# Eight changes of order and form in a two-layer fp32 decoder trunk on one Trainium2 core

## The reference, cut to what matters

```python
# layer 1
h = rmsnorm(x, a_norm) @ a_w_in                  # q, k, v, o of four heads, and 8 gate columns
gates = 15 * tanh((gates + b_gates) / 15); ig, fg = split(gates)
lf = log_sigmoid(fg)                             # = -ln(1 + exp(-fg))
b = cumsum(lf); m = running max                  # stabiliser; rows exp(b - m), exp(-m), decay per chunk
num = (q k^T * exp(D - m)) v + exp(b + m0 - m) * (C q);  C = decay * C + v k^T   # chunk after chunk
x = x + (norm(num / max(|den|, exp(-m))) * sigmoid(o)) @ a_w_out
x = x + swiglu(rmsnorm(x, ffn_norm[0]))
k2, v2 = rmsnorm(x, kv_norm) @ w_kv + b_kv       # one shared K and V, two KV heads
# layer 2
s = q k2^T / 8, band of 128;  p = exp(s - max) / (sum + exp(sink - max));  o = p v2
x = x + o @ b_w_out + b_b_out
x = x + swiglu(rmsnorm(x, ffn_norm[1])); out = rmsnorm(x, final_norm)
```

## Time and profile before

| | before |
|---|---|
| median of 3 runs | 2072.8 us (2071.33 to 2073.25) |
| the profiled execution, its own time | 2074.34 us |
| its span in the trace | 2072.7 us |
| busy in the span: PE / DVE / ACT / POOL | 2019.2 / 1349.9 / 925.3 / 1211.6 us |
| mean granted clock of PE | 0.994 of full speed |
| DMA, mean over the span | 200 GB/s |

### The profile page before, as it was taken

How to read it: one execution, slowest core, us unless ns; L and a number is a source line. 1 busy time by engine, 2 the same in 40 slices (tenths; PEclk the granted TensorE clock), 3 DMA queues, 4 the chain that set the end, 5 groups by cost and what they waited for, 6 DMA issues and landing times.

```text
span 2072.7 us, 29248 instructions
## 1 busy us (share of the span) xinstructions
PE 2019.2 (97%) x9992; PEld 1660.2 (80%) x9992; DVE 1349.9 (65%) x1929; ACT 925.3 (45%) x1951; POOL 1211.6 (58%) x1058
## 2 busy tenths in 40 slices
PE   7899999999999999999999999899999999999998
PEld 6788989878888888888878666588788888888886
DVE  7654652668777777464665677768776676645567
ACT  6444343365545545432344444536545444432233
POOL 5532520664888988565664111264888797756565
PEclk9999999999999999999999999999999999999999
DMA  5655545843777787795844000564567667688673
GB/s 154 194 189 181 184 156 203 304 133 122 254 234 258 238 255 244 252 393 169 269 136 85 28 22 22 203 213 122 176 231 251 226 229 249 213 306 313 203 257 139
DMA packets 295431, 415.03 MB, mean 200 GB/s; under 512 B 40040, under 2 KB 218232, under 8 KB 295296
## 3 DMA queue, kind: packets, MB, share of 16 engines
q1 hardware_dynamic: 260752, 307.87, 45.3%
q10 hardware_dynamic: 33120, 100.68, 13.5%
q0 software_dynamic: 1424, 4.77, 0.8%
HBM read 259.09 MB, written 154.17 MB: 199 GB/s over the span
## 4 chain that ended last, share of the span: by engine, by line
PE 86%; DVE 7%; ACT 3%; issue 2%; DMA 1%; POOL 0%; SPq 0%; ACTq 0%; DVEq 0%; POOLq 0%
PE ps L2216 21%; PE ps L2218 21%; PE ps L2217 21%; PE ps L2119 8%; PE ps L2121 4%; PE ps L2480 1%; PE ps L2339 1%; PE ps L2340 1%; PE ps L2336 1%; PE ps L2271 1%; PE ps L2509 1%; DVE mats L1652 1%; PE ps L2499 1%; DVE forms L1750 1%; PE ps L2385 1%
## 5 line engine op out<-in xcount | busy, mean ns | idle before, releaser
L2216 PE MATMUL ps<-forms,mats 128*128 128x512 f32 x2016 | 789.6, 392 | 5.5 <-ACT part L1302 2.3
L2218 PE MATMUL ps<-forms,mats 128*128 128x512 f32 x2016 | 785.9, 390 | 0.0
L2217 PE MATMUL ps<-forms,mats 128*128 128x512 f32 x2016 | 785.8, 390 | 0.0
L1007 POOL TENSOR_TENSOR mats<-sum_a,mats 128x256 fp32r<-128x256 f32 (+2 forms) x384 | 405.6, 1061 | 365.4 <-ACT mats L1241 364.4
L2216 PEld LDWEIGHTS ps<-forms,mats 128*128 128x128 f32 x2016 | 379.4, 188 | 90.8 <-issue 10.2
L2218 PEld LDWEIGHTS ps<-forms,mats 128*128 128x128 f32 x2016 | 379.3, 188 | 79.2
L2217 PEld LDWEIGHTS ps<-forms,mats 128*128 128x128 f32 x2016 | 379.5, 188 | 77.6
L1675 DVE TENSOR_TENSOR X<-ps,X 128x512 f32<-128x512 f32 x390 | 268.4, 690 | 218.4 <-PE ps L2218 216.1
L1241 ACT ACTIVATE mats<-sum_a 128x256 fp32r<-128x256 f32 (+2 forms) x392 | 201.6, 516 | 324.0 <-PE ps L2218 306.7
L1652 DVE TENSOR_TENSOR mats<-stream_raw,mats 128x256 fp32r<-128x256 f32 (+2 forms) x302 | 277.1, 919 | 18.7 <-ACT mats L1241 18.0
L1241 ACT ACTIVATE mats<-stream_raw 128x256 fp32r<-128x256 f32 (+2 forms) x302 | 156.6, 519 | 249.6 <-PE ps L2218 246.1
(11 more groups left out here) (230 smaller groups left out, 2696.2 us busy)
## 6 DMA issues: line engine op xcount, KB each, us to landing
forms<-scratch_forms ACTq DMA_DIRECT2D x182, 512.0 KB, 5.4
scratch_forms<-prep_forms SPq DMA_DIRECT2D x161, 512.0 KB, 3.5
stream_raw<-in_w_gate_up_dram SPq DMA_DIRECT2D x88, 512.0 KB, 5.4
scratch_forms<-head_forms SPq DMA_DIRECT2D x49, 512.0 KB, 2.6
scratch_hidden<-hidden SPq DMA_DIRECT2D x84, 256.0 KB, 5.5
prep_raw<-in_w_down_dram SPq DMA_DIRECT2D x38, 512.0 KB, 5.7
stream_raw<-scratch_hidden SPq DMA_DIRECT2D x32, 512.0 KB, 4.6
forms<-scratch_forms SPq DMA_DIRECT2D x28, 512.0 KB, 8.1
```

What stands on the lines that cost most here:

```text
L1007: pool.tensor_tensor(blocks(m[:, q, 1, :], it.width), stream_source(it, q), blocks(m[:, q, 0, :].bitcast(F32), it.width), ALU.subtract).th ...
L2216: mm(dst, ah, bh, start=OPENS[q] and k == 0, stop=False, skip_group_check=True)
L2217: mm(dst, ah, bl, start=False, stop=False, skip_group_check=True)
L2218: m = mm(dst, al, bh, start=False, stop=k == w - 1, skip_group_check=True)
```

## The change

1. **Start.** SP issues the eight x tiles in a row, then `a_norm`. The gate columns are issued by ACT's queue ahead of its first activation. ACT and DVE split the gate weights one tile earlier (t == 4 in place of 5).
2. **Gate chain.** The factor 15 of ig moves from DVE to ACT. A DVE `reciprocal` of the 4 x 1024 row `one_plus_exp` takes the place of ACT's Exp(-ln); it no longer waits for ACT's Ln, and an Exp of one column after the Ln loads ACT's table. The split of unit H+3 moves between ACT's Exp and Ln, and two of POOL's three gains move behind later work.
3. **First head.** No form is made behind v tile 5; forms 5 and 6 stand behind v tiles 6 and 7. DVE's low part of form 6 moves into the loop over chunks.
4. **Attention start.** An Exp of one column, ahead of the first query output, loads ACT's table.
5. **Masked copies.** The two become one of 128 x 512, over masks that lie side by side.
6. **Run B.** Its first product (six matmuls) is issued in the last pair, at s == STEPS + 1; `run(1)` goes on from the second.
7. **Seams.** At item 7 `x_normed_of` stands ahead of `stream_hi`, for both halves.
8. **Preparation.** The list `events` loses its first three products: run A spreads 84 forms over 123 products in place of 126, run B 77.

```diff
-        events = [(runs[l][8 + f].n, q) for f in range(2, 20) for q in range(NQ)]
+        events = [(runs[l][8 + f].n, q) for f in range(2, 20) for q in range(NQ)][3:]
@@ SP, start
-            for t in range(3):
+            for t in range(TT):
                 load_x(t)
-            sp.wait_ge(gate_w_cleared, 1)
-            sp.dma_start(gates[:, :, 0:NH_A], win[:, :, g0:g0 + NH_A]).then_inc(gate_w_loaded, 16)
-            sp.dma_start(gates[:, :, 32:32 + NH_A], ...).then_inc(gate_w_loaded, 16)
-            load_gains(0, a_norm[0, :])
-            for t in range(3, TT):
-                load_x(t)
+            sp.dma_start(gcol[:, 0, :], a_norm[0, :].rearrange("(k p) -> p k", p=P), ...).then_inc(a_gain_loaded, 16)
@@ POOL, gates
-            for j in range(3, 6):
-                gain(Unit(U_HEADS + j))
+            gain(Unit(U_HEADS + 3))
...
+            gain(Unit(U_HEADS + 4))
             pool.wait_ge(gate_dve, 10)
             pool.dma_start(scr_negm, negm[:]).then_inc(negm_stored, 16)
             pool.wait_ge(negm_stored, 16)
             load_neg_row(0)
+            gain(Unit(U_HEADS + 5))
@@ ACT, a run at item 7
+                        if i == 7 and q < 2:
+                            x_normed_of(it.seam[0], 2, its[i - 1].group + 4 * q, q)
...
-                            if norm < 4 and pos and q < 2:
+                            if norm < 4 and pos and q < 2 and i != 7:
@@ ACT, start
+            act.wait_ge(gate_w_cleared, 1)
+            act.dma_start(gates[:, :, 0:NH_A], win[:, :, g0:g0 + NH_A]).then_inc(gate_w_loaded, 16)
+            act.dma_start(gates[:, :, 32:32 + NH_A], ...).then_inc(gate_w_loaded, 16)
-                if t == 5:
+                if t == 4:
                     write_hi(Unit(U_GATES))
@@ ACT, gates
             act.activation(enf[:], fg[:], ACT.Exp, scale=-GATE_CAP).then_inc(gate_act, 1)
-            act.wait_ge(gate_dve, 3)
+            write_hi(Unit(U_HEADS + 3))
+            act.wait_ge(gate_dve, 2)
             act.activation(lnu[:], one_enf[:], ACT.Ln).then_inc(gate_act, 1)
-            act.wait_ge(gate_act, 2)
-            act.activation(fg[:], lnu[:], ACT.Exp, scale=-1.0).then_inc(gate_act, 1)
-            write_hi(Unit(U_HEADS + 3))
+            act.activation(table_col[:], neghalf[:, 0:1], ACT.Exp)
+            act.activation(ig[:], ig[:], ACT.Copy, scale=GATE_CAP).then_inc(gate_act, 1)
@@ ACT, first head
-                        if first and t < NQ:
-                            head_row_hi(0, t)
+                        if first and t != 5:
+                            head_row_hi(0, t - t // 6)
@@ DVE, gates
-            dve.tensor_scalar(ig[:], ig[:], GATE_CAP, None, ALU.mult).then_inc(gate_dve, 1)
...
+            dve.reciprocal(fg[:], one_enf[:]).then_inc(gate_dve, 1)
             dve.wait_ge(gate_dve, 4)
-            dve.wait_ge(gate_act, 3)
             dve.tensor_tensor(enf[:], enf[:], fg[:], ALU.mult).then_inc(gate_dve, 1)
             dve.wait_ge(gate_dve, 5)
+            dve.wait_ge(gate_act, 2)
             dve.tensor_tensor(lf[:], enf[:], lnu[:], ALU.subtract).then_inc(gate_dve, 1)
@@ DVE, attention
-                    dve.tensor_tensor(PTc[:, e % 2], pT, cur, ALU.mult).then_inc(pt_ready, 1)
-                    dve.tensor_tensor(PTp[:, e % 2], pT, prv, ALU.mult).then_inc(pt_ready, 1)
+                    dve.tensor_tensor(PT[:, e % 2], pT.unsqueeze(1).to_broadcast([P, 2, 2, P]), keep, ALU.mult
+                                      ).then_inc(pt_ready, 1)
@@ PE, a run and the attention loop
-                    for q in range(NQ):
+                    for q in range(int(l == 1 and local(it) == 0), NQ):
                         product(it, q)
...
+                if s == STEPS + 1:
+                    pe.wait_ge(bank_free[0], uses.before[0])
+                    product(runs[1][0], 0)
```

More of the change, by code:

```diff
@@ L928, in _ @@
             pool.memset(mask_neg[:], 0.0).then_inc(const_step, 1)
[L929 to L930 removed]
+            for t in (keep_le[:], keepT_cur, keepT_prev):
+                pool.memset(t, 1.0).then_inc(const_step, 1)
             pool.wait_ge(const_step, 6)
@@ L1389, in run @@
                     tile_hi(2, 3, 1)
+            act.wait_ge(gate_w_cleared, 1)
+            gates = raw[:, 0, :].rearrange("p (k n) -> p k n", k=KT)
+            g0 = 2 * NH_A * DQK + 2 * D
+            act.dma_start(gates[:, :, 0:NH_A], win[:, :, g0:g0 + NH_A]).then_inc(gate_w_loaded, 16)
+            act.dma_start(gates[:, :, 32:32 + NH_A], win[:, :, g0 + NH_A:g0 + 2 * NH_A]).then_inc(gate_w_loaded, 16)
             K = uses.stage(NORM)
@@ L1980, in head @@
                 if first:
-                    for q in range(3, NQ):
+                    for q in range(3, NQ - 1):
                         head_row_lo(0, q)
@@ L2012, in head @@
                                                      ps[:, b, 0:W1], ALU.mult, ALU.add).then_inc(bank_free[b], 1)
-                    if first and c:
-                        head_row_lo(1, c - 1)
+                    if first:
+                        head_row_lo(int(c > 0), (c - 1) % NQ)
                     if not first and not last and c < NQ:
@@ L2512, in _ @@
                             d = slice(a * DH_B, (a + 1) * DH_B)
-                            m = mm(ps[d, b, 0:P], vb[:, ne - 1, d], PTp[:, e % 2, a], start=False, stop=True)
+                            m = mm(ps[d, b, 0:P], vb[:, ne - 1, d], PT[:, e % 2, 1, a], start=False, stop=True)
                     m.then_inc(oT_ready, 1)
```

39 lines of the change are left out of this document (17 added, 22 removed).

## The result

| | before | changed |
|---|---|---|
| median | 2072.8 us (4 runs, 2071.3 to 2073.3) | 2081.3 us (4 runs, 2080.2 to 2084.5) |
| ratio of the times | | 1.0043, 95% interval 1.0031 to 1.0055 |
| the profiled execution / its span | 2074.34 / 2072.7 us | 2080.24 / 2078.6 us |
| busy PE | 2019.2 us | 2017.4 us |

The changed kernel is 8.6 us slower, where 7.9 less was forecast. Its profiled execution was the fastest of the four, and only 5.9 above that of before. Executions of one kernel spread: the fastest and the slowest lie 2 us apart in one kernel of the experiments (11) and 7.8 in another (1), and further down it is seen where.

A forecast was written before the change was run, and what follows sets the result against it. PE was taken as the bound, busy 2019.2 of 2072.7 us, leaving 53.5 for better order. Eight terms summed to -7.9: 2066.4 us for the profiled execution, 2064.9 as the median, range 2057.5 to 2070.5.

The forecast's parts named there:

- Preparation, -2.3: Runs A and B: forms three products later remove PE's 1.2 us wait for `part` in each run; -2.3 us.
- The late sum: Preparation: ACT stands 4.18 us for POOL's sum of the second prepared form, with PE's awaited copy behind it.
- Rival D: Preparation: closer pitch makes ACT wait for POOL's sum in 23 rows, 1.16 us each; slower, 2092 us; chance 0.05.
- Start, +1.9: Kernel start: `a_norm` behind eight x tiles lands at about 15.1 and delays half 1 of the gate columns; +1.9 us.
- +3.0 for a landing at 16.2: Kernel start: upper end of the start's range, if the gain vector lands at 16.2; +3.0 us.
- v copies, -3.0: First head: last v copy no longer waits behind a form's store, leaving 0.9 of wait for the state; -3.0 us.
- Gate chain, +1.8: Gates: DVE's reciprocal takes 8.4 us, scans end 1.8 later, and PE's gate wait becomes 4.5; +1.8 us.
- The rival with one pass: Gate chain: reciprocal takes one pass, 1.21 us, giving -2.7 in place of +1.8; 2060.4 us in all; chance 0.30.
- Attention start, -1.3: Attention's start: earlier table load may let DVE's scaling go before POOL's long sum; half taken, -1.3 us.
- Masked copies, -1.1: Attention: one merged copy saves 0.066 us a step, counted in the last pair's waits and six small ones; -1.1 us.
- First product, -3.9: Last pair: run B's six matmuls fill PE's gap; second product starts 3.3 ahead, 0.6 less at low clock; -3.9 us.
- Seams, 0: Seams: four forms on ACT still stand ahead of both reordered steps, so the 1.9 us wait, twice, stays; 0.

The follow-up runs named there:

- (11): Changed kernel with the old start, gate reciprocal by ACT's Exp, run A's table rejoining the old one, and form 3's low part earlier: 2066.4 us, 0.9969 to before.
- (1): Changed kernel with the old table of forms, preparation events starting three products earlier again in both runs: 2075.3 us, ratio to before 1.0007.
- table of 7: Changed kernel with run A's forms 1 to 6 at most two products later, then the old table; run B stays shifted: 2071.4 us, 0.9991 to before.
- 10: Kernel before with only run B's first product issued in the last pair: 2069.9 us, ratio to before 0.9986.

## Why the prediction was wrong

The sum of -7.9 became +5.9 in the profiled execution. Three terms are off by 15.6 together (preparation 9.3, start 3.2, v copies 3.1), and the gate chain gives 2.2 back; the rest is under 2.

- **Preparation, -2.3 became +7.0: the step that failed.** The late sum was read rightly, and the two waits for ACT's `part` went in both runs (-1.5 each). But "the pitch falls from 1.50 to 1.46 products a form, so nothing should gather" took the mean for the places. The table puts three forms on three products at six places. At five places of run A, ACT waits 3 to 4.9 for SP's store of the form two before; at two of them, where it waits 4.9 and 4.4 and the store stands behind a burst of loads, PE lost 5.3 and 4.3. Rival D had the mechanism nearly (forms that make ACT wait, with a copy of PE behind), at the wrong resource, POOL's sum in place of SP's store, and in 23 places in place of two. It had 0.05. With the old table the kernel is 6.0 faster than the changed one (1), and with the table of 7 it is 9.9 faster.
- **Start, +1.9 became +5.1 (3.8 in the mean of all).** The three queues stood as forecast. But the sum priced the gain alone, at 15.1. It landed at 15.9, and what held POOL was a load that the sum did not have, the later half of the gate columns, moved to ACT's queue, at 16.3. By the prediction's own +3.0 for a landing at 16.2, 2.1 of the 5.1 are left; beside them stands the clock after PE's 4.8 us of idleness, 0.50 and 0.67 in the two stretches behind it, which I had not counted, although the prediction itself names that price for another place.
- **v copies, -3.0 became +0.1.** The copies came when they should. The next in line was named, the state of chunk 0, and priced at 0.9; but I took it to be bound to DVE's own work. It was bound through two splits to the same store that the v copy had been taken out from behind, and form 6 as such hadn't moved. The second wait, 1.8 behind the load of the next row, was in no term.
- **Gate chain, +1.8 became -0.4.** The mechanism stands, only the sizes were off: 6.53 us where 8.4 was taken, 5.2 ns more an element and not 7, and `one_plus_exp` took 0.68 where 1.2 was taken. So the wait for the gates is 2.2 and not 4.5. The up to 2 us that POOL's split could have added to DVE's second row did not come: that row took 1.21. (The row of 3.30 in the earlier trace rows stood beside a split of POOL, from 44.4 to 47.0, and not beside a product.) The rival with one pass (1.21) is excluded. Against ACT's Exp the reciprocal still loses 2.1. The estimate from the Trainium skill's page "VectorE: DVE Perf Modes" (fixed hardware budget), 8.5, was too high by 2.0, but it was on the right side of one pass.
- **Attention start, -1.3 became -1.5, by luck.** The size came out and the reason didn't: the scaling still ran beside POOL's sum (2.65 us, both at 1165.4). The clock did not fall in that execution, which 10 shows without the edit too. The runs show no worth of the edit apart from that.
- **Masked copies, -1.1 became 0 to -0.3.** Waits that were summed from the list were not on PE's path step by step.
- **First product, -3.9 became -3.8 here and -2.3 in the mean.** The product lies in the gap as forecast, and the second product started where it was put (1347.7 with the kernel 12.0 late, forecast 1335.6). But the rest of the gain was to come at the low clock, and in this execution the clock did not fall at all; at an equal clock 0 to 2.2 are left. That the full size came out here is in part luck.
- **Seams, 0: right** (3.8 before and after, 1.9 each).

The landing of the small loads is seen, but not why the gate columns took 13.6 us beside the x tiles; no run moved them alone, or the gain alone. Open as well is which places of the cut table are bad and why only those.

## What to carry to other kernels

Work that is spread by a table must be looked at place by place against what the other queues issue at fixed places: a mean pitch says nothing. When an edit takes an instruction out from behind a wait, list what still stands behind that wait, on every engine, before booking the gain. And ask whether a row "waits for a store" because of the data or because of the queue that issues it: the time of the issue tells. A gain next to a stretch in which the clock falls in some executions wants several traces.

## What the runs showed of the hardware that was not expected

- A DVE reciprocal of 4 x 1024 took 6.53 us, each time with a split of POOL beside it; a plain operation of that shape took 1.21.
- Two loads of 16 KB, issued at 1.9 and 2.4 us on a second queue beside 4 MB on the first, took 13.2 and 13.9 us to land; on the first queue, between the x tiles, 5.5.
- A store of 512 KB took 3.4 us to land in the median, and 8.3 where it was issued right behind four loads of 512 KB, a stream load and a hidden store.
- Executions of one kernel differ by 2 to 7.8 us, and a part of it has a place: whether PE's granted clock falls in a stretch with waits of about 1.3 us (attention's start: 1.5 us; the last pair: 1.2 us and more, and up to 4 between the extremes). In all seven traces in which PE stood 4.4 to 4.9 us at the start, it was 0.50 in 20 to 25 us.
